# Delta rule: the first four key tiles as seven half-size products, convolved from SBUF

## The chip, the core and the metric

The kernel runs on one core of one Trainium2 chip. The core's engines are TensorE (matmuls, which write PSUM banks), VectorE, ScalarE, GpSimd and SyncE (which here issues most DMAs); the profile calls them PE, DVE, ACT, POOL and SP. They run on their own and wait for each other by semaphores. The metric is the time of one execution on the device in microseconds (us).

## What is computed

Two transformer blocks run one after the other. The change lies in the first, in its bidirectional gated delta rule. The normalised input h (512 tokens, 1024 features) is projected to 1024 query, 1024 key and 1024 value features, each feature is convolved over the tokens with five taps, and SiLU follows. Keys and queries get an L2 norm per head.

```python
h = rms_norm(x, norm_pre[i])
(aq, ak, av, az, dq, dk, dv, db, da, dz, gate_att, gate_dn) = split_cols(h @ w_in[i])
...
qkv = jax.nn.silu(short_conv(jnp.concatenate([dq, dk, dv], axis=-1), conv_w[i]))
cq, ck, cv = qkv[..., :DN_KW], qkv[..., DN_KW:2 * DN_KW], qkv[..., 2 * DN_KW:]
qd = l2_norm(heads(cq, DN_HEADS, DN_DK)) * (DN_DK ** -0.5)
kd = l2_norm(heads(ck, DN_HEADS, DN_DK))
```

## The kernel before

The program is a sequence of stages, each written out by hand for each engine; there is no scheduler, and each engine runs its instructions in the order in which they are written. Three of the stages matter here.

**Stage 1** ends with four products of the attention branch: two units for the gate (`ga`, units U_GA and U_GA + 1) and two for the branch output (`bra`, U_BRA and U_BRA + 1). Each unit takes two weight blocks of 256 columns and is computed as seven products of half size instead of eight (Strassen's scheme in Winograd's form), by the helper `seven`. It needs sums and differences of weight quarters, `parts` and `last_part` on GpSimd, and differences of input quarters, `term_h` for the input h. ScalarE copies two of the half-size results aside (`hold_first`, `hold_third`), VectorE adds them to others (`add_second`, `add_seventh`) and writes the quarters of the result (`recombine`, with `raw22`, `raw12` and `raw21`; the last frees the unit's three PSUM banks).

**Stage 2** is the convolution loop. It goes over 24 tiles j of 128 features, keys first (j = 0 to 7), then queries, then values. For a tile,
- TensorE makes a plain product into one of four banks `psv` (`feature_tile`, eight matmuls of 512 columns),
- ScalarE writes the middle tap from the bank to `conv` (in the text: the first tap),
- VectorE adds the four other taps, reading the bank (four `scalar_tensor_tensor`),
- ScalarE takes SiLU, and for j < 16 the square,
- two tiles later TensorE sums the squares (into a bank of `pss`) and turns the tile to token order (into another bank of `pss`), which is called a pair below; ScalarE evicts both banks.

There are four banks of `pss` as well, in turn: TensorE waits for `free_s` before it writes a bank that ScalarE has not evicted. ScalarE's order within step j is fixed by the code: first tap of tile j, at j = 2 the exponentials of the gates, the evictions of tile j - 2, SiLU of tile j, square of tile j. Two buffers of `conv` alternate.

VectorE has other work between the convolutions: at j = 4 a transpose and two differences, at j = 5 one long operation, at j = 6 `exponents`, at j = 10 and 11 transposes, from j = 12 the inverse of the triangular blocks by elimination (`eliminate`), and transposes at the end. GpSimd does the same elimination for the other direction. Ahead of the loop ScalarE and VectorE compute the gates (an issue of a DMA that saves `mixT`, then three table loads with their functions on ScalarE).

**Stage 3** is the chunkwise recurrence; it starts with results of the last convolution steps.

Of the kernel before, what the change touches and what calls it, by code (L numbers as in the profile page):

```python
# [15 lines left out]
P = 128  # L16
SEQ, DM = 512, 1024
NT = SEQ // P
# [112 lines left out]
def weight_order():  # L131
# [140 lines left out]
def build(nc, a, out, dumps):  # L272
    ctx = ExitStack()
    with ctx:
# [141 lines left out]
        assert top[0] <= D + 16 * K  # L416

# [273 lines left out]
        for what, i in steps:  # L691
            if what == "scores":
# [9 lines left out]
        V_ON = V_CONV + 24 + 3 + (NCK - 1) * 10 + 2  # L702
# [7 lines left out]
        U_Q, U_GA, U_BRA, U_DZ, U_GD, U_BRD, U_WO, U_PLEG, U_KV, U_VP, U_G2, U_QP = (  # L710
            SEVEN.index(k) for k in (("qkv", 0), ("ga", 0), ("bra", 0), ("dz", 0), ("gd", 0), ("brd", 0), ("wo", 0),
# [3 lines left out]
        SEVEN_JOB = [2, 5, 8, V_ATT, V_ATT + 3, V_ATT + 6, V_ATT + 9, V_ON, V_ON + 3, V_ON + 14, V_ON + 17, V_ON + 20, V_ON + 23,  # L715
# [3 lines left out]
        TERM_SET = [("q", 0)] * 3 + [("h", 0)] * 2 + [("h", 1)] * 2 + [("q", 1)] * 4 + [("h", 2)] * 2 + \  # L719
# [27 lines left out]

        def conv_job(j):

            return V_CONV + j + (j >= 2) + (j > 6) + (j > 18)  # L750

        def intra_job(n, hg):

            return V_CONV + 27 + 10 * n + (6 if n < NCK - 1 else 0) + hg
# [99 lines left out]
        def _(pe):  # L854
# [246 lines left out]
            for u in range(U_BRA, U_DZ):  # L1101
                seven(u, oT, part_a, term_o)
# [85 lines left out]
            for j in range(24 + 2):  # L1188
                if j == 2:

                    L.need(s["gg_ready"])
                    o = bank("v")
                    for g in range(2):
                        mm(o[:, g * 32:(g + 1) * 32], tri[g], co_g[:, g * 32:(g + 1) * 32], start=True, stop=True)
                    mm(o[:, 64:128], same, co_g, start=True, stop=True)
                    for x in range(2):
                        m = mm(o[:, 128 + 64 * x:192 + 64 * x], same[:, x * CK:x * CK + 1].broadcast_to([P, P]), co_g,
                               start=True, stop=True)
                    m.then_inc(s["full_v"], 1)
# [9 lines left out]
                i = j - 2  # L1209
                if 0 <= i < 16:  # L1210
# [2267 lines left out]
```

## Time and profile before

| | us |
|---|---|
| median of 3 runs (lowest, highest) | 1453.69 (1449.48, 1455.49) |
| the profiled execution, its own time | 1452.92 |
| its span in the profile | 1450.8 |
| PE busy | 1380.4 (95%) |
| DVE busy | 715.0 (49%) |
| ACT busy | 391.2 (27%) |
| POOL busy | 428.8 (30%) |

The span is 2.1 us shorter than the execution's own time; what lies around it is the same for any edit inside. A busy TensorE is not one at its peak. A timeline row gives start, duration, engine, line, operation, output and inputs with shape, how many instructions were merged (each fp32 matmul is recorded as two), and in brackets the idle time of the engine before it and who ended it. A windows row gives the stretch, its length, for PE, PEld (weight loads), DVE, ACT and POOL the busy time with the number of instructions, then the granted TensorE clock as a share of 2.4 GHz, the share of DMA and GB/s. In a row by shape, the numbers after the bar are total busy us and mean ns of one instruction.

### The profile page before, as it was taken

What the parts mean: (1) busy time and instruction counts of PE and PEld (TensorE: products, weight loads), DVE (VectorE), ACT (ScalarE), POOL (GpSimd) and SP (SyncE); (2) the same over time, 40 slices, a digit from 0 to 9 for tenths busy, and PEclk for the clock granted to TensorE, in tenths of its full rate; (3) what the DMA queues carried; (4) which work ended last, traced back from release to release, by engine and by line L of the source; (5) the groups of instructions that cost most, each with busy time, mean ns of one, the idle gap of its engine ahead of it and who ended that gap; (6) DMA issues with size and microseconds to landing.
All of it is one profiled execution on the core that took longest, in us unless ns stands there. A gap on an engine that the chain in (4) does not pass through costs nothing. (4 is left out here: it accounts for less than half of the span.)

```text
span 1450.8 us, 21812 instructions
## 1 busy us (share of the span) xinstructions
PE 1380.4 (95%) x8394; PEld 948.4 (65%) x8394; DVE 715.0 (49%) x1256; ACT 391.2 (27%) x799; POOL 428.8 (30%) x321
## 2 busy tenths in 40 slices
PE   7999999999999989999999999999999989997886
PEld 5865556886454448877888878878877874332222
DVE  5262562124539987779543333461355464332225
ACT  3313564103343234332120022330354020000003
POOL 3411020720004617565373725133201013221110
PEclk9999999999999999999999999999999989999989
DMA  8226220123111213322514230232224868999995
GB/s 328 86 93 232 93 112 30 60 86 116 59 59 60 86 59 119 129 108 79 226 59 178 87 116 19 98 77 106 97 63 168 325 243 338 418 419 421 422 413 236
DMA packets 48439, 236.57 MB, mean 163 GB/s; under 512 B 12136, under 2 KB 13424, under 8 KB 27601
## 3 DMA queue, kind: packets, MB, share of 16 engines
q1 hardware_dynamic: 42720, 224.54, 39.8%
q0 software_dynamic: 5040, 8.27, 1.6%
q10 hardware_dynamic: 576, 2.36, 0.4%
q8 instruction: 68, 1.11, 0.3%
q14 instruction: 35, 0.28, 0.1%
HBM read 223.72 MB, written 21.51 MB: 169 GB/s over the span
## 5 line engine op out<-in xcount | busy, mean ns | idle before, releaser
L926 PE MATMUL psv<-arena 128*128 128x256 f32 x1648 | 361.2, 379 | 0.2 <-DVE arena L2747 0.2
L926 PEld LDWEIGHTS psv<-arena 128*128 128x128 f32 x1648 | 312.9, 190 | 43.8 <-issue 1.5
L2680 DVE TENSOR_TENSOR arena<-arena,psv 128x512 f32<-128x512 f32 (+1 forms) x99 | 68.6, 693 | 273.5 <-PE psv L926 271.4
L888 PE MATMUL psv<-arena,wslot 128*128 128x512 f32 x384 | 170.7, 598 | 0.0
L1570 PE MATMUL pss<-arena 128*64 128x512 f32 x432 | 121.4, 629 | 14.5 <-DMA arena<-w_expert_in 13.8
L888 PEld LDWEIGHTS psv<-arena,wslot 128*128 128x128 f32 x384 | 71.2, 190 | 83.2 <-issue 82.9
L888 PE MATMUL pss<-arena 128*128 128x512 f32 (+1 forms) x256 | 105.9, 567 | 1.0 <-ACT arena L2048 1.0
L2912 DVE SCALAR_TENSOR_TENSOR arena<-psv,ccols,arena 128x510 f32<-128x510 f32 (+1 forms) x96 | 71.9, 749 | 50.0 <-ACT arena L2104 46.7
L926 PE MATMUL psv<-arena,wslot 128*128 128x256 f32 x384 | 86.3, 380 | 2.3 <-DVE arena L2680 1.3
L1570 PEld LDWEIGHTS pss<-arena 128*64 128x64 f32 x432 | 37.9, 145 | 68.9 <-issue 68.7
L1913 ACT ACTIVATE arena<-pss 128x512 f32<-128x512 f32 (+2 forms) x89 | 51.5, 579 | 112.8 <-PE pss L888 56.2
L926 PEld LDWEIGHTS psv<-arena,wslot 128*128 128x128 f32 x384 | 72.6, 190 | 13.2 <-issue 2.3
L888 PEld LDWEIGHTS pss<-arena 128*128 128x128 f32 x256 | 47.7, 190 | 50.7 <-issue 48.4
L926 PE MATMUL psv<-wslot,arena 128*128 128x256 f32 x320 | 74.3, 387 | 6.2 <-ACT arena L1972 2.7
L2458 POOL TENSOR_TENSOR arena<-wslot 128x1024 f32<-128x1024 f32 x11 | 26.4, 2398 | 172.5 <-PE pss L1077 86.0
L2476 POOL TENSOR_TENSOR arena<-arena 128x1024 f32<-128x1024 f32 x20 | 49.1, 2453 | 81.0 <-DVE arena L2773 35.8
L926 PEld LDWEIGHTS psv<-wslot,arena 128*128 128x128 f32 x320 | 61.5, 194 | 16.5 <-ACT arena L1972 3.9
L3382 DVE TENSOR_TENSOR arena<-pss,arena 128x256 f32<-128x256 f32 x16 | 6.8, 425 | 129.0 <-ACTq L240 129.0
L2677 DVE TENSOR_TENSOR arena<-arena 128x512 f32<-128x512 f32 (+2 forms) x64 | 50.5, 789 | 32.8 <-ACT arena L2060 22.3
L1589 PE MATMUL psv<-arena 128*64 128x512 f32 x236 | 56.5, 614 | 2.9 <-ACTq L240 1.6
L2345 ACT ACTIVATE arena<-pss 128x256 f32<-128x256 f32 x16 | 6.2, 385 | 184.4 <-PE pss L1570 184.4
L2458 POOL TENSOR_TENSOR arena<-arena 128x1024 f32<-128x1024 f32 x10 | 23.9, 2386 | 99.1 <-PE psv L926 99.0
(420 smaller groups left out, 2063.0 us busy)
## 6 DMA issues: line engine op xcount, KB each, us to landing
wslot<-w_blocks SPq DMA_DIRECT2D x56, 1024.0 KB, 5.1
arena<-w_blocks SPq DMA_DIRECT2D x30, 1024.0 KB, 5.8
arena<-w_expert_out SPq DMA_DIRECT2D x29, 1024.0 KB, 25.1
arena<-w_expert_in SPq DMA_DIRECT2D x28, 1024.0 KB, 26.6
arena<-w_expert_in SPq DMA_DIRECT2D x28, 512.0 KB, 8.1
arena<-w_expert_in SPq DMA_DIRECT2D x6, 2048.0 KB, 24.6
y_dram<-arow SPq DMA_DIRECT2D x1, 4096.0 KB
arena<-c_pool SPq DMA_DIRECT2D x4, 1024.0 KB, 9.0
```

The source lines that it names most:

```text
L888: m = mm(o, l, r, start=(n == 0), stop=(n == len(pairs) - 1))
L926: m = mm(o[:, j * HALF_T:(j + 1) * HALF_T], l[:, c, j * P:(j + 1) * P], r[:, c, :], start=new and j == 0 and c == 0, stop=j == 1 and c == ...
L1570: m = mm(o[x * CAP:(x + 1) * CAP, :], xe[:, k, c, x * CAP:(x + 1) * CAP], win[2 * w + x][:, c, :], start=(c == 0), stop=(c == KC - 1))
L1589: m = mm(o[x * CAP:(x + 1) * CAP, :], hidT[:, k, c, x * CAP:(x + 1) * CAP], wout_home(n, x, c)[:, c0:c0 + 512], start=(c == 0), stop=(c == 1))
L1913: L.did(A(dst, src, func, **kw), s[sig] if sig else None, [s["free_s"]])
L2345: L.did(A(sil[:, k, :], pss[:, (q0 + job) % 4, 0:DE], ACT.Silu), None, [s["sil_ready"]])
L2458: L.did(TT(part[0], a21, a22, ALU.add), s["part_ready"])
L2476: L.did(TT(term[n], lo, hi, ALU.subtract), s["term_ready"])
L2677: L.did(V.tensor_tensor(o, x, y, ALU.mult), *sig)
L2680: L.did(V.tensor_tensor(o, x, y, ALU.add), *sig)
L2912: L.did(V.scalar_tensor_tensor(o[:, lo:hi], b[:, lo + m:hi + m], tap(j, k), o[:, lo:hi], ALU.mult, ALU.add), s["conv_ready"] if k == 4 els ...
L3382: L.did(V.tensor_tensor(hid[:, k, :], pss[:, (s0 + job) % 4, DE:2 * DE], sil[:, k, :], ALU.mult), s["hid_ready"], [s["free_s"], s["sil_use ...
```

## The change

The first four key tiles (weight blocks `dqkv` 4 and 5) become one more unit of seven products, U_DK, right behind the four of stage 1. Its result goes to a new tensor in SBUF, `first_keys`, and the convolution of j = 0 to 3 reads it there: first tap on ScalarE and the other four on VectorE. The squares of these four tiles are written over `first_keys`. Since all four tiles are there at once and none of the four convolutions is done while TensorE makes a tile, the pairs of sum and turn move: tiles 0 and 1 at j = 5, tiles 2, 3 and 4 at j = 6, from tile 5 on again two steps later. ScalarE's evictions of them move to the same steps. The input differences `term_h` of the gate are used again, and GpSimd forms the weight sums of the unit after those of U_BRA + 1. ScalarE runs `hold_first` of the unit ahead of the save of `mixT` and of its gate functions. The weight blocks `dqkv` 4 to 7 go through four slots instead of two.

```diff
@@ weight_order
+    for b in (4, 5, 6, 7):
+        stream(("dqkv", b), "w_in", O_DQ + b * WC, WC)
     slot_group.append((len(blocks), 4))
-    for b in (4, 5, 6, 7, 0, 1, 2, 3, 8, 9, 10, 11):
+    for b in (0, 1, 2, 3, 8, 9, 10, 11):
         stream(("dqkv", b), "w_in", O_DQ + b * WC, WC)
@@ helpers
+        first_keys = at(B + 64 * K, 4, SEQ)
...
+        def corner_k(v, u, j, n):
+
+            return v[:, 2 * j:2 * j + 2, n * HALF_T:(n + 1) * HALF_T]
+
         def conv_job(j):
 
-            return V_CONV + j + (j >= 2) + (j > 6) + (j > 18)
+            return V_CONV + j + (j > 6) + (j > 18)
+
+        def keys_turned_at(j):
+
+            return {4: (), 5: (0, 1), 6: (2, 3, 4), 7: (5,)}.get(j, (j - 2,))
@@ TensorE
-            for j in range(24 + 2):
-                if j == 2:
-
-                    L.need(s["gg_ready"])
...
+            seven(U_DK, hT, part_a, term_h)
+            L.need(s["gg_ready"])
...
+            for j in range(4, 24 + 2):
...
-                i = j - 2
-                if 0 <= i < 16:
-                    L.need(s["sq_ready"])
-                    o = bank("s")
...
+                for i in keys_turned_at(j):
+                    if i < 16:
+                        L.need(s["sq_ready"])
+                        o = bank("s")
+                        squared = first_keys[:, i, :] if i < 4 else csq[:, i % 2, :]
...
+                    if i < 8 or i >= 16:
+                        pe.wait_ge(s["silu_ready"], i + 1)
+                        turn_chunks(kT[:, i, :] if i < 8 else cst[:, i % 2, :])
@@ ScalarE
             phase(1)
+            hold_first(U_DK, held_a)
             act.dma_start(mix_dram.rearrange("(p n) -> p n", p=P), mixT.rearrange("p c n -> p (c n)"))\
                 .then_inc(s["mix_kept"], 16)
...
+            hold_third(U_DK, held_a)
+            corner_of(U_DK, first_keys, ACT.Copy, corner_k)
+            act.wait_ge(s["raw_ready"], 3 * (U_DK + 1))
             for j in range(24 + 2):
-                if j < 24:
+                if j < 4:
+                    L.did(A(conv[:, j % 2, :], first_keys[:, j, :], ACT.Copy, scale=tap(j, 2)), s["tap_ready"])
+                elif j < 24:
                     act.wait_ge(s["full_v"], conv_job(j) + 1)
...
-                i = j - 2
-                if 0 <= i < 16:
-                    evict(dn_sum[:, i, :], NT, "sum_ready")
...
+                for i in keys_turned_at(j) if j >= 4 else ():
+                    if i < 16:
+                        evict(dn_sum[:, i, :], NT, "sum_ready")
...
                 if j < 16:
-                    L.did(A(csq[:, j % 2, :], dst, ACT.Square), s["sq_ready"])
+                    L.did(A(first_keys[:, j, :] if j < 4 else csq[:, j % 2, :], dst, ACT.Square), s["sq_ready"])
@@ GpSimd
-            for u in range(U_BRA, U_DZ):
+            for u in range(U_BRA, U_DK + 1):
                 parts(u, part_a)
                 last_part(u, part_a)
@@ VectorE
+            add_second(U_DK, held_a)
+            recombine(U_DK, held_a, first_keys, corner_k)
             for j in range(24):
...
-                b = full()
+                b = first_keys[:, j, :] if j < 4 else full()
```

**TensorE.** Before, the pairs lie between tiles, one behind each. These rows begin with the tile of j = 2 (L888), then sum (L1215) and turn (L980) of key tile 0, and so on; `free_s` is the wait for an evicted bank of `pss`.

```order
L888 MATMUL psv<-arena,wslot 128x512 [waits free_v,ld_w1]
L888 MATMUL psv<-arena,wslot 128x512 x7
L1215 MATMUL pss<-const,arena 64x1 [waits free_s,sq_ready]
L1215 MATMUL pss<-const,arena 64x1 x7
L980 MATMUL pss<-const,arena 64x128 [waits free_s,silu_ready]
L980 MATMUL pss<-const,arena 64x128 x7
L888 MATMUL psv<-arena,wslot 128x512 [waits free_v]
L888 MATMUL psv<-arena,wslot 128x512 x7
L1215 MATMUL pss<-const,arena 64x1 [waits free_s,sq_ready]
L1215 MATMUL pss<-const,arena 64x1 x7
L980 MATMUL pss<-const,arena 64x128 [waits free_s,silu_ready]
L980 MATMUL pss<-const,arena 64x128 x7
```

Now the pairs come in bunches. The rows begin with the turn of key tile 1 at j = 5 (L992), then the tile of j = 6 (L900), then sum (L1228) and turn of key tiles 2 and 3; the pair of tile 4 follows.

```order
L992 MATMUL pss<-const,arena 64x128 [waits free_s,silu_ready]
L992 MATMUL pss<-const,arena 64x128 x7
L900 MATMUL psv<-arena 128x512 [waits free_v,ld_w2]
L900 MATMUL psv<-arena 128x512 x7
L1228 MATMUL pss<-const,arena 64x1 [waits free_s,sq_ready]
L1228 MATMUL pss<-const,arena 64x1 x7
L992 MATMUL pss<-const,arena 64x128 [waits free_s,silu_ready]
L992 MATMUL pss<-const,arena 64x128 x7
L1228 MATMUL pss<-const,arena 64x1 [waits free_s,sq_ready]
L1228 MATMUL pss<-const,arena 64x1 x7
L992 MATMUL pss<-const,arena 64x128 [waits free_s,silu_ready]
L992 MATMUL pss<-const,arena 64x128 x7
```

What moved: six banks of `pss` are wanted in a row behind tile 6, after four behind tile 5, with no tile between the three pairs.

**ScalarE.** Before, step j = 2: first tap (L2104), the table load and exponentials of the gates (L2107, L2108), eviction of sum and turn of tile 0 (L1913), table load, SiLU and square (L2136, L2138), and the first tap and evictions of j = 3.

```order
L2104 ACTIVATE arena<-psv,ccols 128x512 [waits full_v,sq_ready]
L2107 ACT_TABLE_LOAD [waits gG_ready]
L2107 ACTIVATE arena<-arena 128x64 [waits tap_ready]
L2108 ACTIVATE arena<-arena 128x192 [waits chain_s]
L1913 ACTIVATE small<-pss 128x4 [waits full_s,ga_ready]
L1913 ACTIVATE arena<-pss 128x4x128 [waits sum_ready,full_s]
L2136 ACT_TABLE_LOAD [waits chain_s]
L2136 ACTIVATE arena<-arena 128x512 [waits conv_ready]
L2138 ACTIVATE arena<-arena 128x512 [waits silu_ready]
L2104 ACTIVATE arena<-psv,ccols 128x512 [waits full_v,sq_ready]
L1913 ACTIVATE small<-pss 128x4 [waits full_s,tap_ready]
L1913 ACTIVATE arena<-pss 128x4x128 [waits sum_ready,full_s]
```

Now the rows begin at j = 2 behind the exponentials: table load and SiLU (L2155), square (L2157), then the steps j = 3 and 4 with the first tap from SBUF (L2120) or a bank (L2123), and the first tap of j = 5 with the first two evictions (L1926).

```order
L2155 ACT_TABLE_LOAD [waits conv_ready]
L2155 ACTIVATE arena<-arena 128x512 [waits ga_ready]
L2157 ACTIVATE arena<-arena 128x512 [waits silu_ready]
L2120 ACTIVATE arena<-arena,ccols 128x512 [waits sq_ready]
L2155 ACTIVATE arena<-arena 128x512 [waits conv_ready,tap_ready]
L2157 ACTIVATE arena<-arena 128x512 [waits silu_ready]
L2123 ACTIVATE arena<-psv,ccols 128x512 [waits full_v,sq_ready]
L2155 ACTIVATE arena<-arena 128x512 [waits conv_ready,tap_ready]
L2157 ACTIVATE arena<-arena 128x512 [waits silu_ready]
L2123 ACTIVATE arena<-psv,ccols 128x512 [waits full_v,sq_ready]
L1926 ACTIVATE small<-pss 128x4 [waits full_s,tap_ready]
L1926 ACTIVATE arena<-pss 128x4x128 [waits sum_ready,full_s]
```

What moved: no eviction stands ahead of the first tap of j = 5 any more, and the table load of j = 2 now carries the wait for `conv_ready` (the end of VectorE's part of the convolution), where before it carried the wait for ScalarE's own eviction.

## Rows read from the trace of the kernel before

**Rows 1.** Windows: us, busy time by engine, granted clock, DMA share, GB/s.

```profile
432.00:540.00 108.00, 106.96 (x530) 51.45 (x530) 99.33 (x137) 34.14 (x57) 46.06 (x70) 1.00 0.19 69
```

**Rows 2.** Timeline of TensorE, where the convolution stage begins and ends.

```profile
337.05 13.90 PE L888 MATMUL psv<-arena,wslot 128*128 128x512 f32 x32
350.79 0.53 PE L1194 MATMUL psv<-arena,const 128*128 128x32 f32 x4
...
351.85 7.08 PE L888 MATMUL psv<-arena,wslot 128*128 128x512 f32 x16
...
360.35 7.13 PE L888 MATMUL psv<-arena,wslot 128*128 128x512 f32 x16
...
394.57 1.13 PE L1111 MATMUL psv<-arena,const 128*128 128x512 f32 x2
395.54 7.03 PE L888 MATMUL psv<-arena,wslot 128*128 128x512 f32 x16
...
539.11 1.09 PE L980 MATMUL pss<-const,arena 128*64 128x128 f32 x16 [1.04 <-ACT arena L2136]
```

**Rows 3.** Timeline of VectorE: end of attention, gates, convolution.

```profile
313.15 0.69 DVE L2680 TENSOR_TENSOR arena<-arena,psv 128x512 f32<-128x512 f32 x1
...
337.32 0.69 DVE L2680 TENSOR_TENSOR arena<-arena,psv 128x512 f32<-128x512 f32 x1 [2.04 <-PE psv L926]
...
345.82 0.39 DVE L2897 COPY arena<-arena 64x32 f32<-64x32 f32 x2
...
352.84 3.10 DVE L2912 SCALAR_TENSOR_TENSOR arena<-psv,ccols,arena 128x510 f32<-128x510 f32 x4 [3.49 <-ACT arena L2104]
...
380.47 2.48 DVE L2919 TENSOR_TENSOR arena<-arena 128x1024 f32<-128x1024 f32 x2
...
388.78 2.29 DVE L2922 SCALAR_TENSOR_TENSOR arena<-arena 128x2048 f32<-128x2048 f32 x1 [0.15 <-DVE arena L2912]
...
448.13 3.10 DVE L2912 SCALAR_TENSOR_TENSOR arena<-psv,ccols,arena 128x510 f32<-128x510 f32 x4 [0.44 <-ACT arena L2104]
...
461.68 3.10 DVE L2912 SCALAR_TENSOR_TENSOR arena<-psv,ccols,arena 128x510 f32<-128x510 f32 x4
```

**Rows 4.** Timeline of ScalarE, the same stretch.

```profile
338.94 0.34 ACTq L2071 DMA_DIRECT2D mix_dram<-arena  x1
...
349.43 1.28 ACT L2136 ACT_TABLE_LOAD   x1 [4.38 <-DVE arena L2912]
...
352.05 0.69 ACT L2104 ACTIVATE arena<-psv,ccols 128x512 f32<-128x512 f32 x1
356.04 0.63 ACT L2136 ACTIVATE arena<-arena 128x512 f32<-128x512 f32 x1 [3.30 <-DVE arena L2912]
...
361.71 0.17 ACT L1913 ACTIVATE small<-pss 128x4 f32<-128x4 f32 x1
...
362.70 1.28 ACT L2136 ACT_TABLE_LOAD   x1
```

**Rows 5.** Groups of instructions by shape: busy us, mean ns, idle before.

```profile
L2912 DVE SCALAR_TENSOR_TENSOR arena<-psv,ccols,arena 128x510 f32<-128x510 f32 x48 | 35.9, 749 | 48.3 <-ACT arena L2104 46.7 <-DVE arena L2863 0.2 <-DVE arena L2677 0.2
...
L3247 DVE SCALAR_TENSOR_TENSOR arena<-arena,cols 128x512 f32<-128x512 f32 x4 | 3.0, 751 | 6.4 <-ACT arena L2318 6.4
...
L2267 ACT ACTIVATE arena<-arena,const 128x512 f32<-128x512 f32 x4 | 2.9, 722 | 0.1
```

**Rows 6.** Timeline of TensorE around two waits for expert weights.

```profile
1309.24 7.09 PE L1570 MATMUL pss<-arena 128*64 128x512 f32 x32 [2.86 <-DMA arena<-w_expert_in]
...
1326.06 1.11 PE L1570 MATMUL pss<-wslot,arena 128*64 128x512 f32 x1 [4.62 <-DMA arena<-w_expert_in]
```

**Rows 7.** Windows of 2 us around the second of these waits.

```profile
1308.00:1310.00 2.00, 0.76 (x4) 0.35 (x6) 0.00 (x0) 0.00 (x0) 1.08 (x2) 1.00 1.00 418
1324.00:1326.00 2.00, 0.00 (x0) 0.00 (x0) 0.00 (x0) 0.00 (x0) 1.01 (x1) 0.62 1.04 434
...
1330.00:1332.00 2.00, 2.00 (x8) 0.57 (x6) 0.00 (x0) 0.00 (x0) 0.00 (x0) 0.67 1.05 424
```

More of the change, by code:

```diff
@@ L1100, in _ @@
             L.need(s["oz_ready"], KC)
-            for u in range(U_BRA, U_DZ):
+            for u in range(U_BRA, U_DK):
                 seven(u, oT, part_a, term_o)
@@ L1186, in intra @@
                 m.then_inc(s["full_v"], 1)
-            for j in range(24 + 2):
-                if j == 2:
-                    L.need(s["gg_ready"])
[L1192 to L1199, printed above, removed]
+            seven(U_DK, hT, part_a, term_h)
+            L.need(s["gg_ready"])
+            o = bank("v")
+            for g in range(2):
+                mm(o[:, g * 32:(g + 1) * 32], tri[g], co_g[:, g * 32:(g + 1) * 32], start=True, stop=True)
+            mm(o[:, 64:128], same, co_g, start=True, stop=True)
+            for x in range(2):
+                m = mm(o[:, 128 + 64 * x:192 + 64 * x], same[:, x * CK:x * CK + 1].broadcast_to([P, P]), co_g,
+                       start=True, stop=True)
+            m.then_inc(s["full_v"], 1)
+            for j in range(4, 24 + 2):
                 if j < 24:
@@ L1207, in _ @@
                         used("v", dqkv)
-                i = j - 2
-                if 0 <= i < 16:
-                    L.need(s["sq_ready"])
-                    o = bank("s")
-                    for q in range(NT):
-                        for x in range(2):
-                            m = mm(o[HX[x], q:q + 1], csq[:, i % 2, chunk(q, x)], ones[:, 0:1], start=True, stop=True)
-                    m.then_inc(s["full_s"], 1)
-                if 0 <= i < 8 or i >= 16:
-                    pe.wait_ge(s["silu_ready"], i + 1)
-                    turn_chunks(kT[:, i, :] if i < 8 else cst[:, i % 2, :])
+                for i in keys_turned_at(j):
[3 more added lines that the diff above has]
+                        squared = first_keys[:, i, :] if i < 4 else csq[:, i % 2, :]
+                        for q in range(NT):
+                            for x in range(2):
+                                m = mm(o[HX[x], q:q + 1], squared[:, chunk(q, x)], ones[:, 0:1], start=True, stop=True)
+                        m.then_inc(s["full_s"], 1)
+                    if i < 8 or i >= 16:
+                        pe.wait_ge(s["silu_ready"], i + 1)
+                        turn_chunks(kT[:, i, :] if i < 8 else cst[:, i % 2, :])
                 if j == 23:
@@ L2066, in _ @@
                 others_of(u, gates, ACT.Sigmoid, "gate_ready")
-            for u in range(U_BRA, U_DZ):
+            for u in range(U_BRA, U_DK):
                 hold_first(u, held_a)
@@ L2492, in _ @@
                 terms(oT, term_o, n)
-            for u in range(U_BRA, U_DZ):
+            for u in range(U_BRA, U_DK + 1):
                 parts(u, part_a)
@@ L2833, in _ @@
             L.need(s["gate_ready"], 2)
-            for u in range(U_BRA, U_DZ):
+            for u in range(U_BRA, U_DK):
                 g, o = [[[corner(v, u, j, n) for n in range(2)] for j in range(2)] for v in (gates, mixT)]
@@ L2913, in _ @@
                                                  ALU.mult, ALU.add),
-                          s["conv_ready"] if k == 4 else None, [s["free_v"]] if k == 4 else [])
+                          s["conv_ready"] if k == 4 else None, [s["free_v"]] if k == 4 and j >= 4 else [])
                 if j == 4:
```

21 lines of the change are left out of this document (11 added, 10 removed), and 1 row of the table SEVEN.

## Prediction

> **What bounds the kernel now.** I read the page first: TensorE is busy for 95% of the span, so an edit counts where it shortens or delays TensorE's order of work, or where another engine leads. Then the timelines of TensorE, VectorE and ScalarE over the convolution loop and the stretch ahead of it, then one windows row. The reader should see two regimes. From 337.05, the first tile's start, TensorE runs without a wait as far as the tile of j = 7 (395.54) and beyond; the stage's first wait in its timeline is the one at 539.11, and that is for a SiLU of ScalarE (L2136), which follows the last convolution [rows 2]. VectorE has long pauses early (3.49 us ahead of j = 1), but j = 12 starts at 448.13 after only 0.44 of idle, and j = 13 at 461.68 with none: 10.45 us of the inverse lie between [rows 3]. From 432 to 540 VectorE is busy 99.33 of 108 us [rows 1]. So up to j = 12 TensorE's tiles set the pace, and from there VectorE's string of work ends the stage. What shifts TensorE at the tiles 7 to 12 shifts the stage's end, and the recurrence behind it, by the same amount. I find no later stretch that waits for a clock of its own: weights are sent for when buffers come free.
>
> **What it removes.** Four tiles take 4 x 6.87 = 27.48 us (two of them 350.79 - 337.05 = 13.74) [rows 2]. A unit of seven takes 24.17, the distance of the last additions of two units in a row (313.15, 337.32) [rows 3]. That is 3.31 less. A pair behind a tile costs 360.35 - 351.85 - 6.87 = 1.63, the gate sums 351.85 - 350.79 = 1.06, `grow` 0.97 [rows 2]. If TensorE never waits, it reaches the tile of j = 7 after 24.17 + 1.06 + 3 x 6.87 + 2 x 1.63 + 3 x 1.5 + 0.97, which is 54.6 us after 337.05, against 58.5 before: **3.9 us earlier** (pairs in a row save the small gap behind a tile). I take 1.5 for them; 1.63 would make it 3.5.
>
> **What it adds and moves.** The convolutions 0 to 3 no longer overlap their own tiles. They start when the last quarter of `first_keys` is written: 337.32 + 24.17 + 0.69 = 362.18, so ScalarE's first tap of j = 0 begins at about 362.25, where before it had done j = 0 and 1 by then. From there the loop is a strict string: tap, four additions, SiLU, square, next tap, since ScalarE's order is fixed. From tap to SiLU is 356.04 - 352.05 = 3.99; SiLU and square take 352.05 - 349.43 = 2.62 less the table load of 1.28 and its gap, so 1.32 [rows 4]. A step is **5.31 us**. It was hidden behind tile and pair (8.50); now it is not.
> - From SBUF instead of PSUM: the additions took 749 ns on a bank; the nearest row with two SBUF inputs and a column as the factor (L3247, 512 columns) has 751. ScalarE's `Copy` with a factor took 0.69 from a bank [rows 4]; L2267 from SBUF has 722 ns [rows 5]. So 5.34 for the four SBUF steps.
> - Table loads: at j = 0 the load waits for the convolution, before as now (349.43). At j = 2 it ran before under the convolution (362.70, behind the evictions); in the new order it carries the wait for `conv_ready`, so both steps cost 1.28 + 0.02 more. The gate's exponentials, a load of 1.28 and two activations on fewer columns than the tap's 0.69, come to at most 2.7 and lie under VectorE's 3.10.
>
> The first tap of j = 5 thus starts at 362.25 + 4 x 5.34 + 5.31 + 2 x 1.30 = **391.5**. Only behind it, in ScalarE's order, does the first eviction of a key sum stand: 0.69 + 0.17 and gaps, 392.4. TensorE, meanwhile, does tiles 4 and 5, the pairs of keys 0 and 1 (which fill the four `pss` banks), and tile 6: 337.05 + 24.17 + 1.06 + 3 x 6.87 + 2 x 1.63 = **386.15**. Its next instruction, the sum of key 2, needs a freed bank: a **wait of some 6.3 us**, until 392.5. The pairs of keys 2 and 3 follow the four evictions (0.99 us a pair [rows 4], so hardly slower than TensorE) and end near 395.7. The sum of key 4 needs the eviction of key 2's sum, in step 6. VectorE, with j = 4 done at 390.1, does the 2.48 of differences and a transpose first [rows 3] and convolves j = 5 from 393.0 to 396.1; SiLU, square, tap and eviction bring 398.5: a **second wait of 2.8 us**. Then the pair (1.6) and `grow` (0.97) let tile 7 start at 401.2.
>
> 401.2 against 395.54 is **5.7 us later**. As a sum: -3.9 of work, +6.3 and +2.8 of waits, +0.5 of gaps and of the slower pair of key 4. Tile 7 has its bank (j = 4's was freed at 390), and the 2.29 of j = 5 on VectorE ends near 398.5, in time for j = 6. From tile 7 on everything stands as before, each step led by TensorE until j = 12, so nothing gives the 5.7 back.
>
> **What I cost at nothing.** `hold_first` of the unit ahead of the gates: the first half-size product ends at 337.05 + 24.17 / 7 = 340.5, so the DMA moves from 338.94 to about 341.4 and the gates' last copy from 346.2 to 348.7 [rows 3, 4]. Behind it `add_second` is done at 349.5; TensorE wants it for its fifth half-size product at 350.9. The cover is 1.4 us; past it the delay would be TensorE's one for one. The gate sums wait for nothing, at 361.2. GpSimd forms the weight sums in time in which it stood idle, and the two weight blocks are sent for when the slots of U_BRA's come free, one unit ahead. If they were late, the unit's second product would wait; the two units before, in the same pattern, did not.
>
> The profiled execution had 1452.92 by its own time, 0.8 under the median of the runs shown. 1452.92 + 5.7 = 1458.6; to the median, **1459.4**.
>
> **A rule on the source.** The rows say that a source in SBUF costs the additions the same (749 and 751 ns) [rows 5]. The Trainium skill (VectorE: DVE Perf Modes, section on the TRN2 errata) gives VectorE a fixed part of 58 cycles for an SBUF source and 120 for PSUM. By that table, an estimate, sixteen additions would be 16 x 62 cycles at 0.96 GHz = 1.0 us quicker and the forecast 1458.4; no row here bears it out.
>
> **The rivals.** Bounds of the forecast case itself: the load of j = 2 hidden after all gives 4.4, and pairs at 1.63 with 0.1 us more of signalling on each of the six steps give 6.7; so 1457.5 to 1461, chance **0.58**.
>
> 1. **The clock.** After TensorE's idle 2.86 us the granted clock stayed at 1.00; after 4.62 it had fallen to the 1.2 GHz level before work resumed at 1326.06, and came back near 1331.3 (0.67 over 1330 to 1332), 5.2 us later [rows 6, 7]. The first wait here is 6.3. Half rate from 392.5 to 397.7 would stretch 3.2 us of pairs to about 5.8, to 398.3, and the second wait swallows that, so I put no cost in the sum. If the second wait or the small matmuls keep the clock down for another 5.2 us, 2.6 are lost: +8.3, **1462.0**. For it: three pairs are small products. Against: the clock did not fall after 2.86 us alone. Chance **0.17**. The Trainium skill (TensorE: Matmul & The Clock Gate, on HAM oscillation) states that idle gaps of TensorE bring the gated clock back; the trace agrees with that for the longer gap, and by it alone the fall at the first wait is certain.
> 2. **Faster: no wait at the banks.** If the evictions of step 5 were done by 386.15, TensorE's work alone would count: -3.9, **1449.8**. That needs the first tap of j = 5 at 385.3 instead of 391.5, a step of 4.1 us instead of 5.3. Each us that the string is shorter gives back about one, so the time crosses "before" at a string 5.7 us shorter. The durations leave no room for it; only an error in my reading of ScalarE's order would. Chance **0.12**.
> 3. **The delay is taken up later.** Between j = 7 and j = 12 TensorE would have to make up time, or the inverse on VectorE to start on something else than j = 12. Then the end of the stage moves by less: -1 to +2, about **1454**. For it: ScalarE's and VectorE's pauses up to j = 9. Against: TensorE has none in which to gain. Chance **0.13**.
>
> **From cases to numbers.** Nearly all cases lie within 0.5% (7.3 us), which is about what a measurement of this kernel can tell from no change; past it lie most of rival 1 and the upper edge of the forecast: slower by over 0.5% 0.20, within 0.5% 0.77, faster 0.03. The range leaves out rival 2 and the tail of rival 1: 1452 to 1463.
>
> **What the profile after would show.** Right: TensorE idle for 5 to 7 us before the sum of key 2, released by ScalarE, and 2 to 3 us before that of key 4; a granted clock of about 0.5 in part of the five us behind the first; steps of 5.3 us on VectorE for j = 0 to 4 with two of 6.6; tile 7 near 401; the wait for the last SiLU (539.11 before) some 5.7 us later. Wrong: a string step under 4.5 us, an additions' row well off 750 ns from SBUF, a wait inside the unit of seven (gates or weight sums late), or a stage's end that does not follow tile 7.

## The result and the profile after

The median went from 1453.45 us (7 runs, 1449.46 to 1455.49) to **1457.47 us** (7 runs, 1455.96 to 1458.00): ratio 1.0025, 95% interval 1.0016 to 1.0034. That is slower by 3.6 (by the ratio) to 4.0 us (by the medians), inside "no change" as the prediction drew it (within 0.5%), 1.9 us under its number and at the lower edge of its main case (1457.5 to 1461). The profiled execution took 1457.05 us, its span 1455.2.

TensorE in the timeline, from the gate sums (L1204) to tile 7 (L900 at 402.26), and at the stage's end; these rows answer to [rows 2]:

```profile
362.26 0.53 PE L1204 MATMUL psv<-arena,const 128*128 128x32 f32 x4
...
363.45 13.97 PE L900 MATMUL psv<-arena,wslot 128*128 128x512 f32 x32
...
380.19 7.13 PE L900 MATMUL psv<-arena 128*128 128x512 f32 x16
393.57 1.02 PE L1228 MATMUL pss<-const,arena 128*64 128x1 f32 x16 [6.26 <-ACTq L242]
394.42 1.98 PE L992 MATMUL pss<-const,arena 128*64 128x128 f32 x16
396.16 0.99 PE L1228 MATMUL pss<-const,arena 128*64 128x1 f32 x16
396.98 1.56 PE L992 MATMUL pss<-const,arena 128*64 128x128 f32 x16
399.56 0.63 PE L1228 MATMUL pss<-const,arena 128*64 128x1 f32 x16 [1.03 <-ACTq L242]
...
402.26 2.31 PE L900 MATMUL psv<-arena 128*128 128x512 f32 x5
...
545.82 1.09 PE L992 MATMUL pss<-const,arena 128*64 128x128 f32 x16 [1.02 <-ACT arena L2155]
```

TensorE waits nowhere up to tile 6. Then it waits 6.26 us before the sum of key 2 and 1.03 before that of key 4; ScalarE ended both waits. VectorE's rows say why; they answer to [rows 3] (338.36 is the last addition of the unit ahead, 362.56 that of U_DK, L2933 the convolution):

```profile
338.36 0.69 DVE L2699 TENSOR_TENSOR arena<-arena,psv 128x512 f32<-128x512 f32 x1 [0.51 <-PE psv L938]
...
362.56 0.69 DVE L2699 TENSOR_TENSOR arena<-arena,psv 128x512 f32<-128x512 f32 x1 [2.77 <-PE psv L938]
364.10 3.11 DVE L2933 SCALAR_TENSOR_TENSOR arena<-arena,ccols 128x510 f32<-128x510 f32 x4 [0.85 <-ACT arena L2120]
370.73 3.11 DVE L2933 SCALAR_TENSOR_TENSOR arena<-arena,ccols 128x510 f32<-128x510 f32 x4 [3.52 <-ACT arena L2120]
...
376.00 3.11 DVE L2933 SCALAR_TENSOR_TENSOR arena<-arena,ccols 128x510 f32<-128x510 f32 x4 [1.33 <-ACT arena L2120]
382.63 3.11 DVE L2933 SCALAR_TENSOR_TENSOR arena<-arena,ccols 128x510 f32<-128x510 f32 x4 [3.52 <-ACT arena L2120]
387.97 3.10 DVE L2933 SCALAR_TENSOR_TENSOR arena<-psv,ccols,arena 128x510 f32<-128x510 f32 x4 [2.24 <-ACT arena L2123]
```

The starts lie 6.63, 5.27, 6.63 and 5.34 us apart: a string in which VectorE and ScalarE take turns, with a table load in two of the steps (VectorE's three short operations behind the second convolution fit into its pause). ScalarE's rows show the load that waits, and the first eviction behind the tap of j = 5 (they answer to [rows 4]):

```profile
379.19 1.28 ACT L2155 ACT_TABLE_LOAD   x1 [1.26 <-DVE arena L2933]
...
392.49 0.69 ACT L2123 ACTIVATE arena<-psv,ccols 128x512 f32<-128x512 f32 x1
393.21 0.17 ACT L1926 ACTIVATE small<-pss 128x4 f32<-128x4 f32 x1
```

The windows of 2 us around the first wait (the clock is the third number from the end):

```profile
388.00:390.00 2.00, 0.00 (x0) 0.00 (x0) 1.93 (x3) 0.00 (x0) 0.00 (x0) 1.00 0.00 0
390.00:392.00 2.00, 0.00 (x0) 0.00 (x0) 1.78 (x4) 0.80 (x2) 0.00 (x0) 0.78 0.00 0
392.00:394.00 2.00, 0.42 (x9) 0.46 (x10) 1.95 (x2) 1.82 (x4) 0.00 (x0) 0.50 0.00 0
394.00:396.00 2.00, 2.00 (x28) 2.00 (x28) 1.91 (x3) 0.87 (x3) 0.00 (x0) 0.50 0.00 0
396.00:398.00 2.00, 2.00 (x30) 2.00 (x28) 1.81 (x3) 0.81 (x2) 0.00 (x0) 0.51 0.00 0
398.00:400.00 2.00, 0.97 (x25) 0.76 (x22) 1.97 (x2) 1.82 (x4) 0.00 (x0) 1.00 0.00 0
```

**Where the time is.** The stretch ahead of the stage ended 1.04 us later in this execution (VectorE 338.36 against 337.32 [rows 3]); three executions of the kernel before differ there by up to 1.2, so it is not the change's. The unit of seven takes 24.17 us, so it began at 362.26 - 24.17 = 338.09, and the stage lasts to 545.82: 207.73, against 539.11 - 337.05 = 202.06 [rows 2]. The stage grew by **5.67 us**. The spans differ by 4.4, which is 1.04 + 5.67 - 2.31: what lies behind the stage took 909.38 us instead of 911.69. So two questions are left: does the string make the waits, and what gave 2.3 us back?

### The profile page after: what moved, and what is told of

Read it like the earlier page. It is cut to its first block and busy times, and to the rows that moved or that the text cites. A ratio compares the mean times of both kernels' runs of the same rounds, so it can differ in the third digit from the quotient of the medians.

```text
span 1455.2 us, 21927 instructions
## 1 busy us (share of the span) xinstructions
PE 1381.6 (95%) x8442; PEld 963.0 (66%) x8442; DVE 718.7 (49%) x1261; ACT 392.9 (27%) x802; POOL 437.3 (30%) x325
## 5 line engine op out<-in xcount | busy, mean ns | idle before, releaser
L938 PE MATMUL psv<-arena 128*128 128x256 f32 x1728 | 378.5, 379 | 0.0
L938 PEld LDWEIGHTS psv<-arena 128*128 128x128 f32 x1728 | 328.2, 190 | 45.4 <-issue 1.0
L900 PE MATMUL psv<-arena,wslot 128*128 128x512 f32 x288 | 128.1, 598 | 0.0
L900 PE MATMUL pss<-arena 128*128 128x512 f32 (+1 forms) x256 | 105.9, 567 | 1.0 <-ACT arena L2061 1.0
L938 PE MATMUL psv<-arena,wslot 128*128 128x256 f32 x416 | 93.6, 380 | 2.3 <-DVE arena L2699 1.3
L900 PEld LDWEIGHTS psv<-arena,wslot 128*128 128x128 f32 x288 | 53.3, 190 | 62.0 <-issue 61.6
L938 PEld LDWEIGHTS psv<-arena,wslot 128*128 128x128 f32 x416 | 78.7, 190 | 14.0 <-issue 2.3
L1926 ACT ACTIVATE arena<-pss 128x512 f32<-128x512 f32 (+2 forms) x89 | 51.5, 578 | 112.0 <-PE pss L900 56.2
L900 PEld LDWEIGHTS pss<-arena 128*128 128x128 f32 x256 | 47.7, 190 | 50.7 <-issue 48.4
L2933 DVE SCALAR_TENSOR_TENSOR arena<-psv,ccols,arena 128x510 f32<-128x510 f32 (+1 forms) x80 | 59.9, 749 | 30.2 <-ACT arena L2123 27.2
L2495 POOL TENSOR_TENSOR arena<-arena 128x1024 f32<-128x1024 f32 x20 | 49.1, 2453 | 81.0 <-DVE arena L2792 35.8
L2699 DVE TENSOR_TENSOR arena<-arena 128x512 f32<-128x512 f32 (+3 forms) x64 | 52.8, 826 | 2.9
```

What stands on the lines that cost most here:

```text
L900: m = mm(o, l, r, start=(n == 0), stop=(n == len(pairs) - 1))
L938: m = mm(o[:, j * HALF_T:(j + 1) * HALF_T], l[:, c, j * P:(j + 1) * P], r[:, c, :], start=new and j == 0 and c == 0, stop=j == 1 and c == ...
L1926: L.did(A(dst, src, func, **kw), s[sig] if sig else None, [s["free_s"]])
L2495: L.did(TT(term[n], lo, hi, ALU.subtract), s["term_ready"])
L2699: L.did(V.tensor_tensor(o, x, y, ALU.add), *sig)
L2933: L.did(V.scalar_tensor_tensor(o[:, lo:hi], b[:, lo + m:hi + m], tap(j, k), o[:, lo:hi], ALU.mult, ALU.add), s["conv_ready"] if k == 4 els ...
```

## Experiments

The "shift" is the stage's length against before. The stage starts 24.17 us ahead of the gate sums (13.74 in the old order, where two plain tiles stand there) and ends with the wait for the last SiLU. "Behind" is what lies between that end and the span's. Both are of one profiled execution each. The times are medians, the ratios those to the kernel before, run on the same chip beside them (its medians: 1454.05 for again to exp_at_5, 1454.38 for tap_ahead to hold_clock, 1453.56 for bank_more and before_late, 1454.07 for before_banks).

| kernel | shift | behind | median | ratio, interval |
|---|---|---|---|---|
| again (the change itself) | +5.67 | 909.33 | 1456.93 | 1.0016 [1.0007, 1.0025] |
| early_evict | +1.26 | 910.35 | 1453.08 | 0.9995 [0.9986, 1.0004] |
| pairs_two | -2.86 | 908.76 | 1448.58 | 0.9970 [0.9957, 0.9984] |
| exp_at_5 | -4.20 | 909.40 | 1446.61 | 0.9949 [0.9936, 0.9963] |
| tap_ahead | -4.17 | 909.99 | 1447.74 | 0.9952 [0.9938, 0.9965] |
| early_hold | -0.38 | 912.15 | 1450.37 | 0.9980 [0.9970, 0.9989] |
| hold_clock | +8.45 | 909.25 | 1458.93 | 1.0031 [1.0019, 1.0044] |
| bank_more | +7.67 | 911.77 | 1460.12 | 1.0045 [1.0033, 1.0057] |
| before_late | +5.60 | 912.77 | 1459.21 | 1.0035 [1.0022, 1.0047] |
| before_banks | +0.65 | 914.83 | 1456.56 | 1.0015 [1.0006, 1.0025] |
| before_again | +0.03 | 911.63 | one run, 1453.14 | |
| before_third | -0.01 | 913.58 | one run, 1455.98 | |

**again** repeats the change.

> The changed kernel once more, to see how much of the time is in the convolution stage and how much in the expert stage behind it. Theory (TensorE waits for pss banks whose evictions stand behind the serial string): tile 7 and the stage's last wait again stand 5.6 to 5.8 us later relative to TensorE's last product of stage 1 than before the change, in any execution; the whole time differs from before by 3 to 6 us, and what is missing from 5.7 lies behind 1300 us, where the waits for expert weights end with or without a fall of the clock. Rival (the stage gives part of the 5.7 back before it ends): the distance from the last product of stage 1 to the wait for the last SiLU grows by 4 us or less.

It reproduced the stage to 0.01 us (waits of 6.26 and 0.88), and the medians differ by 2.9 us, just under the 3 to 6 expected.

**early_evict** takes the evictions out from behind the string, with TensorE's order as it was: ScalarE evicts a bank one or two steps earlier than the pairs' own table says.

```diff
+        def keys_evicted_at(j):
+            return {4: (0, 1), 5: (2, 3), 6: (4,), 7: (5,)}.get(j, (j - 2,))
-                for i in keys_turned_at(j) if j >= 4 else ():
+                for i in keys_evicted_at(j) if j >= 4 else ():
```

> TensorE's order as in the change; ScalarE alone evicts the pairs of keys 0 and 1 at j = 4 (behind the first tap of tile 4), 2 and 3 at j = 5, 4 at j = 6. Theory of the banks: the first wait falls from 6.3 us to about 1 (first tap of j = 4, then the eviction), a wait of 2 to 3 us is left for the square of key 4, tile 7 starts about 6 us earlier than in the change, so the time is that of before within 1 us (-6 to the change), and the clock does not fall. Rival (TensorE waits for the squares, not for the banks): both waits stay and nothing moves. Rival (the loss is the price of the convolutions from SBUF or of the gates): nothing moves.

```profile
388.18 0.63 PE L1232 MATMUL pss<-const,arena 128*64 128x1 f32 x16 [0.92 <-ACTq L242]
...
393.46 0.63 PE L1232 MATMUL pss<-const,arena 128*64 128x1 f32 x16 [2.13 <-ACTq L242]
394.17 1.70 PE L996 MATMUL pss<-const,arena 128*64 128x128 f32 x16
395.81 2.08 PE L1127 MATMUL psv<-arena,const 128*128 128x512 f32 x2
```

In TensorE's timeline the first wait fell from 6.26 to 0.92: the place of the evictions had made it. The stage is 4.4 us shorter than the change's, not 6. The expectation that the clock stays up failed, and the rest lies there: the granted clock was 0.63 over 394 to 396 and 0.52 over 396 to 398, and the turn took 1.70 us and `grow` 2.08, against 1.09 and 1.12 at full clock.

**pairs_two** also moves the pair of key 4 from j = 6 to j = 7, so that only two pairs follow tile 6; the squares of tiles 4 to 7 then go to `first_keys` as well, on ScalarE as on TensorE.

```diff
-            return {4: (), 5: (0, 1), 6: (2, 3, 4), 7: (5,)}.get(j, (j - 2,))
+            return {4: (), 5: (0, 1), 6: (2, 3), 7: (4, 5)}.get(j, (j - 2,))
+            (evictions) {4: (0, 1), 5: (2, 3), 6: (), 7: (4, 5)}
-                        squared = first_keys[:, i, :] if i < 4 else csq[:, i % 2, :]
+                        squared = first_keys[:, i % 4, :] if i < 8 else csq[:, i % 2, :]
...
```

> As early_evict, and the pair of key 4 moves behind tile 7, where its square is long done: pairs 2 and 3 at j = 6, 4 and 5 at j = 7; the squares of keys 4 to 7 go to first_keys too, so that key 4's is not overwritten. Theory: one wait of about 1 us is left, tile 7's successor starts 2.8 us earlier than before the change, VectorE's j = 12 too, and the time is 2 to 3 us under before (8.5 under the change). Rival (VectorE's and ScalarE's string up to j = 7 is the bound whatever TensorE does): no better than early_evict.

One wait of 0.92 us is left, the clock stays up, and tile 7 starts at 391.63. The stage is 2.86 us shorter than before, as expected; the time is lower by 4.4 us (by the ratio), where 2 to 3 were expected, so the rest came from behind the stage.

**exp_at_5** is pairs_two with the gates' exponentials moved from j = 2 to j = 5, behind the string:

```diff
-                if j == 2:
+                if j == 5:
```

> As pairs_two, and ScalarE's exponentials of the gates move from j = 2 to j = 5, where VectorE's differences hold up the convolution anyway and evictions stand between them and the SiLU. Theory (the table load of j = 2 waits for the convolution and costs 1.3 us of the string): the string of j = 2 takes 5.3 instead of 6.6, the last wait of 1 us goes, time 1 us under pairs_two (3.5 to 4 under before). Rival (the load is hidden or the string no longer matters once the banks come early): the same time as pairs_two.

No wait is left, and the stage is 4.20 us shorter than before. The exponentials and the table load behind them cost 1.3 us of stage while they stood in the string (from -2.86 to -4.20). The time is 7.4 us under before, where 3.5 to 4 were expected: again the stage came out as expected and the time did better.

**tap_ahead** leaves the order of pairs and evictions as the change has it and cuts the string instead: ScalarE writes the first tap of j + 1 before it waits for the convolution of j.

```diff
+            first_tap(0)
             for j in range(24 + 2):
-                (first tap of j)
+                if j < 5:
+                    first_tap(j + 1)
+                elif j > 5:
+                    first_tap(j)
```

> The changed kernel with one edit on ScalarE: for j = 0 to 4 the first tap of tile j + 1 stands ahead of SiLU and square of tile j (conv has two buffers). Pairs, evictions and TensorE's order are those of the change. Theory (the string tap, additions, SiLU, square, tap is what makes the evictions late): VectorE's convolutions 0 to 4 follow each other in 3.2 to 4 us instead of 5.3 to 6.6, the first eviction comes about 8 us earlier, both waits of TensorE vanish, the stage ends about 4 us earlier than before the change and the time is about 10 us under the change, like exp_at_5. Rival (evictions must be moved, the string's length is not the matter): the first wait stays above 3 us. Rival (convolving from SBUF is dear by itself): additions slow down when packed, gain under 3 us.

VectorE's rows show the convolutions 0 and 1, and 2 and 3, with no pause between:

```profile
363.53 6.25 DVE L2940 SCALAR_TENSOR_TENSOR arena<-arena,ccols 128x510 f32<-128x510 f32 x8 [0.85 <-ACT arena L2120]
...
370.77 6.25 DVE L2940 SCALAR_TENSOR_TENSOR arena<-arena,ccols 128x510 f32<-128x510 f32 x8
```

TensorE waits nowhere up to tile 7, at 391.86, and the stage is 4.17 shorter. So two ways out, by the order of pairs, evictions and exponentials or by the string's length, come to the same place: the 3.9 us of work that the prediction put down as saved, and 0.3 more, because the three pairs behind tile 6 took 4.22 us (386.68 to 390.90) where 4.5 had been put.

**early_hold** and **hold_clock** ask about the clock. They add idle products (256 columns, 0.44 us each, which the result doesn't use) where TensorE waited: early_hold 2 and 4 of them to early_evict, ahead of the pairs and of the pair of key 4; hold_clock 14 to the changed kernel, ahead of the pairs.

```diff
+                if j == 6:
+                    hold("v", 14)
```

> early_evict with 2 idle products (256 columns, result unused) ahead of its first wait and 4 ahead of its second, which keep TensorE active. In early_evict the granted clock was low from about 394 to 397.6, behind waits of 0.92 and 2.13 us, and the pair of key 4 and grow took 1.6 us longer than at full clock. Theory (the fall of the clock costs early_evict about 1.7 us of the 5.7 that it should have won): clock 1.00 throughout, stage end 1.5 to 2 us earlier against the gate sums than in early_evict (179.15 us from gate sums to the wait for the last SiLU there, 177.3 to 177.6 here). Rival (the waits grow by what the clock gives): no difference.

> The changed kernel with 14 such idle products (6 us) at the head of its first wait. Clock 1.00 throughout. Theory (the fall of the clock in the changed kernel is swallowed by the second wait): the wait for the first eviction ends when it did, pairs 2 and 3 take 3.1 us instead of 4.9, the second wait grows from 0.9 to about 2.8, tile 7 starts within 0.4 us of where it did against the gate sums (40.0 us behind them), time as the change within 1 us. Rival 1 of the prediction (the clock stays down behind the second wait and costs up to 2.6): tile 7 and the stage end 1 us or more earlier.

In early_hold the clock stayed at 1.00, `grow` took 1.12, and the stage was 1.6 us shorter than early_evict's: the part that was missing there was the clock's. hold_clock missed its expectation (tile 7 within 0.4 us of the change's, clock up throughout). Its first two pairs ran at full speed, as meant, so the second wait came out at the forecast's 2.8 us, and the clock fell behind that one:

```profile
393.93 0.63 PE L1230 MATMUL pss<-const,arena 128*64 128x1 f32 x16 [0.22 <-ACTq L242]
...
399.91 1.02 PE L1230 MATMUL pss<-const,arena 128*64 128x1 f32 x16 [2.84 <-ACTq L242]
400.76 1.99 PE L992 MATMUL pss<-const,arena 128*64 128x128 f32 x16
402.68 2.08 PE L1123 MATMUL psv<-arena,const 128*128 128x512 f32 x2
404.54 1.86 PE L900 MATMUL psv<-arena 128*128 128x512 f32 x2
```

Its stage is 2.8 us longer than the change's. That is about rival 1's price (2.6); but the clock was up before this wait and fell in it, where rival 1 had it stay down from the first.

**bank_more, before_late, before_banks** ask what gave 2.3 us back behind the stage. Each adds idle instructions only (and the job numbers that go with them). bank_more is the change with one job more in the rotating `psv` banks (a product of 64 columns, and on VectorE a copy of one column that frees the bank); before_late the kernel before with a delay (13 idle products of 256 columns; its expectation says 512, but the time that it puts, 0.43 us each, fits: the 13 took 5.7 us); before_banks the kernel before with three jobs more, which puts its later jobs into the change's banks.

```diff
(bank_more, behind the gate sums; before_banks the same at j = 3, 5 and 8)
+            mm(bank("v")[:, 0:64], same, co_g, start=True, stop=True).then_inc(s["full_v"], 1)
...
(before_late)
+                if j == 6:
+                    hold("v", 13)
```

> The changed kernel with one idle job more behind the gate sums, in the sequence of the rotating PSUM banks: one product of 64 columns on TensorE and one copy of a single column on VectorE, so that every later job uses the bank that it has in the kernel before. Nothing else changes. In the changed kernels run so far, what lies behind the end of the convolution stage took about 909.8 us in the mean, in three executions of the kernel before 912.3. Theory A, the banks: which bank a job has decides what waits for what in the later stages, and the two and a half us come from there; then this kernel shows 911.6 to 913.6 us behind the stage, its stage stays at about 183.6 us, and its time is some 2 us above the changed kernel, 1459 to 1460. Theory B, the phase of the clock and of the landings: the banks have no part in it; then 908.8 to 911 us behind the stage and a time within 0.6 us of the changed kernel's, 1457 to 1457.8.

> The kernel before with 13 idle products of 512 columns on TensorE behind tile 6 of the convolution stage: 13 times about 0.43 us at full clock is a delay of 5.6 us and nothing else, about as large as the one that the change makes, with the clock kept up. Theory A, a delay goes through in full: the stage and the time both grow by 5.6 us, to about 1459.7, a ratio of 1.0039. Theory B, whatever lies behind the stage takes part of a delay back (the loads of the expert weights do not wait for TensorE, and the clock's low stretches fall elsewhere): the stage grows by 5.6 us, what lies behind it shrinks from about 912.3 to about 909.8, and the time grows by 3 to 4 us, to 1457 to 1458.

> The kernel before with three idle jobs in the sequence of the rotating PSUM banks, ahead of the tiles j = 3, 5 and 8: each one product of 64 columns on TensorE and a copy of one column on VectorE. Three jobs more shift every later job to the bank that it has in the changed kernel (which has one job fewer, and there are four banks), and the convolution stage is otherwise that of before. What was found so far: behind the stage the kernel before took 911.7, 911.6, 913.6 us, and 912.8 with a pure delay; changed kernels with the banks shifted 908.8 to 910.4 (eight, one of them 912.2), and 911.8 with the banks put back. Theory A, the banks: the shift itself gives 2 to 2.5 us back behind the stage. Then this kernel's stage is 188.3 to 188.7 us, what lies behind it 909 to 910.4, and the time 2 us under before, a ratio of 0.9986. Theory B, chance in where the clock's low stretches and the landings of weights fall: 911.5 to 913.6 us behind the stage, and a ratio of 1.0000 to 1.0003.

before_late: the stage grew by 5.60 and the median by 5.65, and what lies behind took 912.77, within the kernel before's own 911.6 to 913.6. By these numbers a delay as such passes through and gives nothing back; the interval of its ratio is wide (+3.2 to +6.8 us). bank_more came out where the theory of the banks had it (911.77), but its stage had grown by 2.0 more: the clock was still at the lower level in the pair of key 4 (1.98) and in `grow` (2.08), so its time (1460.12, where 1459 to 1460 stood for the banks and 1457 to 1457.8 against) says nothing for or against that theory. before_banks then contradicts it: 914.83 behind the stage where the theory wanted 909 to 910.4, and a time 2.2 us above before's by the ratio, where it wanted 2 under (one of its 11 executions took 8106 us; it is in neither median nor ratio). The banks alone don't give anything back.

**before_again and before_third** are the kernel before, profiled twice more, to see how far one kernel's profiles differ.

> The kernel before, profiled again. In its first profile the stretch from the first expert product to the end took 248.9 us, in the eight profiles of changed kernels 244.9 to 248.2; behind the last wait for expert weights the granted clock was low (17.7 us from that product to the product L1667, against 14.8 in the changed kernel). Theory (the clock's fall there hangs on how the DMA landings and TensorE's waits fall in one execution, and the stage's 5.7 us are lost in full): the stretch comes out anywhere from 245 to 249 here too; the convolution stage takes 202.06 from the first tile to the wait for the last SiLU, as in the first profile. Rival (the kernel before is always in the slow pattern there, so that the change gives 2 to 3 us back in the expert stage): 248 to 249.5 again, and 17 to 18 us behind the last wait for weights.

> The same once more, for the spread: theory and rival as for before_again.

The stage repeats to 0.04 us; what lies behind it varies by 2 (a third execution beside these took 1457.12 us). The piece behind the last wait for weights took 14.8 us in both, so the rival of the two expectations, that the kernel before always loses 17 to 18 there, is wrong. The stretch from the first expert product to the end took 246.4 and 249.2 us, against 248.9 in the first profile.

## Why the prediction was right, and where it was off

**The string: right.** Steps of 5.27 and 5.34 with two of 6.63 (forecast 5.34 and 6.6); the first tap of j = 5 at 392.49, less the 1.04 of the late start 391.45 (391.5). The load of j = 2 did wait for `conv_ready`. exp_at_5 and tap_ahead show by removal what the forecast had as argument. The terms put at nothing held too: less the 1.04, the save of `mixT` was issued at 341.41 (forecast 341.4), the gates' last copy ended at 348.69 (348.7) and `add_second` at 349.41 (349.5), and TensorE waited nowhere inside the unit.

**Source in SBUF: right, by the rows.** Groups of the changed kernel by shape: busy us and mean ns.

```profile
L2933 DVE SCALAR_TENSOR_TENSOR arena<-psv,ccols,arena 128x510 f32<-128x510 f32 x40 | 29.9, 749 | 28.8 <-ACT arena L2123 27.2 <-DVE arena L2882 0.2 <-DVE arena L2696 0.2
...
L2933 DVE SCALAR_TENSOR_TENSOR arena<-arena,ccols 128x510 f32<-128x510 f32 x8 | 6.0, 750 | 9.4 <-ACT arena L2120 9.2
```

749 ns from a bank, 750 from SBUF: no difference. The Trainium skill (VectorE: DVE Perf Modes, the TRN2 errata) by its table gives the SBUF source 62 cycles less; the rows differ from it, and the measurement decides.

**The first wait: right**, 6.26 for 6.3, and early_evict shows that the place of the evictions makes it.

**The second wait and the clock: right in the sum.** The clock went to the 1.2 GHz level in the first wait and was back at about 398, 4.4 us after work resumed (5.2 in rival 1's working). The pairs of keys 2 and 3 took 4.97 us (393.57 to 398.54) where 3.2 had been put (5.8 in rival 1's working), and the second wait shrank from 2.8 to 1.03; the forecast had said that it swallows the difference. The Trainium skill (TensorE: Matmul & The Clock Gate, HAM oscillation) has idle gaps bring the gated clock back, and by this trace they do. Rival 1 itself (down for longer) didn't occur here, but in bank_more, whose stage has only 0.2 us of work more, and whose waits ended within 0.02 us of the change's (reckoned from the gate sums), it did: the granted clock fell about half a us earlier, stayed at 0.50 up to 402 and cost 2.0 us. Which of the two an execution gets, these runs don't explain.

**Tile 7: right.** 402.26 - 395.54 - 1.04 = 5.68, forecast 5.7. The stage's end followed it (5.67).

**What failed is the last step, "nothing gives the 5.7 back".** By the medians 1.7 us of it (in again 2.8) are gone. Not by rival 3, which looked between j = 7 and j = 12: the shift is the same at tile 7 and at the stage's end. In the profiled pair the gain lies in the expert stage. Two timelines of TensorE from the last wait for expert weights to the product behind them (`const,arow`), first the kernel before:

```profile
1397.12 9.98 PE L1570 MATMUL pss<-arena 128*64 128x512 f32 x32 [4.33 <-DMA arena<-w_expert_in]
...
1409.54 5.35 PE L1589 MATMUL psv<-arena 128*64 128x512 f32 x16 [0.79 <-ACTq L240]
1414.82 0.66 PE L1667 MATMUL pss<-const,arow 128*128 128x128 f32 x4
```

and the changed kernel (with two windows of the clock of each, as above):

```profile
1404.60 8.78 PE L1583 MATMUL pss<-arena 128*64 128x512 f32 x32 [2.56 <-DMA arena<-w_expert_in]
...
1415.84 3.65 PE L1602 MATMUL psv<-arena 128*64 128x512 f32 x16 [0.82 <-ACTq L242]
1419.43 0.66 PE L1680 MATMUL pss<-const,arow 128*128 128x128 f32 x4
```

```profile
1401.00:1403.00 2.00, 2.00 (x6) 0.48 (x4) 0.00 (x0) 0.00 (x0) 1.22 (x2) 0.50 1.02 412
...
1411.00:1413.00 2.00, 2.00 (x8) 0.74 (x6) 0.00 (x0) 0.00 (x0) 0.00 (x0) 0.50 0.99 379
```

```profile
1408.00:1410.00 2.00, 2.00 (x12) 0.65 (x10) 0.00 (x0) 0.00 (x0) 0.00 (x0) 0.92 1.04 418
...
1416.00:1418.00 2.00, 2.00 (x10) 0.63 (x10) 0.18 (x1) 0.00 (x0) 0.00 (x0) 1.00 0.99 395
```

This piece took 17.70 us there, 14.83 here, for the same products: 9.98 against 8.78 and 5.35 against 3.65 is the clock. Before, it was down from ahead of 1397 to 1403 and again from about 1410 to 1413; in the changed kernel it was down from about 1405 to 1408 and then up. The wait itself ended 0.77 later after the stage's end (1397.12 - 539.11 = 858.01; 1404.60 - 545.82 = 858.78), so 2.10 of the 2.31 lie in this piece.

Over all runs the same piece took 13.1 us behind a last wait of 1.3 or 1.4 (hold_clock, pairs_two), 14.6 to 14.8 behind 2.2 to 2.6 (eight executions), and 15.5 to 17.8 behind 4.3 (four). In eight of nine profiles of the change and its variants the piece took at most 15.5; before_late had 17.80. Yet in before_again and before_third the wait was 2.55 and 2.27 and the piece 14.8, and there the wait ended 1.5 to 2.2 us later instead (860.3 and 861.0 after the stage's end).

Part of the spread arises ahead of the expert weights: the stage's first product in the expert part (L1556 before, 1195.55; L1569 after, 1203.74) came 656.4 us behind the convolution stage's end in the kernel before's first profile, 659.5 and 658.0 in its other two, 657.1 to 658.1 in eight of the changed kernels and 659.4 in bank_more.

So the clock's part is shown for the profiled pair. By the medians, too, the changed program is some 2 us quicker outside the stage: the growth of the median less the shift is -1.1 to -3.9 for the change, its repeat and its seven variants, 0.0 for before_late and +1.8 for before_banks. (A few tenths of this can come from outside the span: an execution took 1.8 to 2.5 us more than its span in these profiles, and not always the same, as is put ahead of the prediction.) **Why its loads and waits fall more kindly stays open**. The banks alone are excluded as the cause, and before_late speaks against a delay. Not tried are the order in which the weight slots are handed on, and the place of the new tensor.

The result lies in the middle of the forecast's range, 1452 to 1463: the stage's 5.7 us were foreseen, that the time came out 1.9 under the number was not. A term for the spread of what lies behind the stage (2 us between profiles of one kernel) belonged in the forecast beside the 5.7.

## What to carry to other kernels

When a consumer loop loses the producer that it ran beside, time it as a string: every hand-over between two engines is then on the path, and so is whatever stands in the slower engine's order, evictions above all. Look first at what else that engine could issue before it waits (here one tap ahead): by the medians that turned +4.0 us into -6.6, and a new order of pairs, evictions and exponentials into -7.4; by the stage alone it is +5.7 into -4.2 for both. And price a saving at the point where TensorE is next held up, with the clock that a wait leaves behind it.

## What the runs showed of the hardware

- The length of one wait does not tell whether the clock falls. Behind 2.86 us alone it stayed up [rows 6, 7]; behind 2.84 in hold_clock, after three us of small products, it fell (turn 1.99, `grow` 2.08), and in early_evict behind 0.92 and 2.13 with small products between. The small products needn't be the reason: behind 2.56 us after large ones it fell as well (the changed kernel at 1404.60; 0.50 over 1406 to 1408).
- Nor do the products ahead of the wait tell. In the expert stage early_evict and hold_clock run the same four groups, with durations equal to 0.01 us, ahead of waits of 2.88 and 2.87 us; in the first the clock was down behind the wait (0.50 over 1364 to 1366), in the second up (1.00 from 1370 on). The last group and the one behind the wait, first early_evict, then hold_clock:

```profile
1356.04 3.65 PE L1606 MATMUL psv<-arena 128*64 128x512 f32 x16
1362.58 8.78 PE L1587 MATMUL pss<-arena 128*64 128x512 f32 x32 [2.88 <-DMA arena<-w_expert_in]
```

```profile
1364.20 3.65 PE L1604 MATMUL psv<-arena 128*64 128x512 f32 x16
1370.72 7.09 PE L1585 MATMUL pss<-arena 128*64 128x512 f32 x32 [2.87 <-DMA arena<-w_expert_in]
```

- Filling a wait with idle products kept the clock up in early_hold (1.6 us of stage, and a ratio of 0.9980 against 0.9995). In hold_clock the fall came in the next wait instead. Each of the two is one profile.
- Six waits for expert weights end at nearly the same distance from the stage's end whatever the variant of the change (the first of them at 770.5 to 771.5 us, the last at 858.3 to 859.3; 772.7 and 860.4 in bank_more), and a DMA ended each of them: there the loads set the pace, and a faster TensorE waits longer. In the kernel before and its variants the last ended at 858.0 to 863.0.
